# A quarter of the descriptor ring for GpSimd's transfers, and three more places for gathered rows

## The reference, cut to what matters

```python
def peer_ffn(x, w_pq, sub_keys, u_emb, v_emb):
    ...
        q = (xc @ w_pq).reshape(c, PEER_HEADS, 2, PEER_HALF)
        s = jnp.einsum('chpd,hpkd->chpk', q, sub_keys).astype(jnp.float32)
        sv, si = lax.top_k(s, PEER_TOPK)
        ...
        cv, ci = lax.top_k(cand, PEER_TOPK)
        eid = jnp.take_along_axis(cid, ci, axis=-1)
        gate = jax.nn.softmax(cv, axis=-1)
        act = jax.nn.gelu(jnp.einsum('chkd,cd->chk', u_emb[eid], xc), approximate=False)
        return jnp.einsum('chk,chkd->cd', (gate * act.astype(jnp.float32)).astype(xc.dtype), v_emb[eid])
```

## Time and profile before

| what | value |
|---|---|
| median of 3 runs | 1012.64 us (1012.56 to 1013.12) |
| span of the profiled execution | 1080.4 us |
| busy: PE, DVE, ACT, GpSimd | 69%, 64%, 37%, 58% of the span |
| TensorE clock granted, mean | 0.819 of full speed |
| read from HBM | 378.16 MB |
| first gather issued, last gather issued | 119.1 us, 1067.8 us |

### The profile page before, as it was taken

One profiled execution on the slowest core, in us unless ns is written; L12 is line 12 of the kernel. 1 busy time (PEld: TensorE's weight loads), 2 busy tenths in 40 slices (PEclk: granted clock), 3 DMA queues, 4 the chain that ended last, 5 costly groups with the idle time before them and its releaser, 6 DMA issues.

```text
span 1080.4 us, 13828 instructions
## 1 busy us (share of the span) xinstructions
PE 742.8 (69%) x4217; PEld 379.1 (35%) x4217; DVE 686.7 (64%) x1725; ACT 404.0 (37%) x1154; POOL 622.1 (58%) x584
## 2 busy tenths in 40 slices
PE   8999986554798677766536768757637567765444
PEld 3575834111354435543212233323213235231111
DVE  1363776997288543698695559988974535639542
ACT  1162142332356470333223346354516742322412
POOL 0000275777667765475565656766775665667664
PEclk9999997877778899988867878877778878887656
DMA  9924699999979999999899999999998999999997
GB/s 364 331 79 184 217 349 411 411 360 377 336 252 359 348 400 412 398 379 379 278 314 325 373 388 353 391 362 362 407 412 308 411 417 416 414 411 409 382 376 270
DMA packets 122443, 381.54 MB, mean 353 GB/s; under 512 B 16026, under 2 KB 40682, under 8 KB 117122
## 3 DMA queue, kind: packets, MB, share of 16 engines
q0 software_dynamic: 83696, 304.81, 74.0%
q1 hardware_dynamic: 38578, 75.78, 19.2%
q10 hardware_dynamic: 96, 0.07, 0.0%
HBM read 378.16 MB, written 4.14 MB: 354 GB/s over the span
## 4 chain that ended last, share of the span: by engine, by line
PE 28%; DVE 19%; issue 17%; ACT 10%; another core or an unknown queue 9%; DMA 8%; POOL 6%; SPq 3%; ACTq 0%; POOLq 0%; DVEq 0%
PE bank L463 17%; PE acc L463 9%; DVE rows L1453 6%; DMA w_uq_sb<-in_w_uq 3%; PE bank L466 3%; POOL rows L1978 3%; DMA rows<-in_peer_v,eid 2%; POOL rows L1996 2%; ACT spread L1101 2%; ACT L1092 1%; SPq L2069 1%; DVE shared L1793 1%; DVE shared L1782 1%; ACT shared L1063 1%
## 5 line engine op out<-in xcount | busy, mean ns | idle before, releaser
L463 PE MATMUL acc<-rows,spread 128*64 128x512 f32 (+1 forms) x1124 | 329.3, 682 | 143.9 <-ACT spread L1101 51.9
L1978 POOL DMA_INDIRECT rows<-in_peer_v,eid x254 | 275.8, 1086 | 160.5 <-issue 66.6
L1996 POOL DMA_INDIRECT rows<-in_peer_u,eid x184 | 193.2, 1050 | 109.0 <-issue 54.7
L463 PEld LDWEIGHTS acc<-rows,spread 128*64 128x64 f32 (+1 forms) x1124 | 89.1, 156 | 310.3 <-issue 240.2
L1453 DVE CUSTOM_DVE_ANT_0 rows<-rows,xr_even 128x1024 f32<-128x1024 f32 x89 | 108.1, 1218 | 34.0 <-DMA rows<-in_peer_u,eid 26.4
L1453 DVE CUSTOM_DVE_ANT_0 rows<-rows,xr_odd 128x1024 f32<-128x1024 f32 x95 | 116.2, 1223 | 19.6 <-DMA rows<-in_peer_u,eid 18.8
L1101 ACT ACTIVATE spread<-wide_consts,wts 128x64 f32<-128x64 f32 (+1 forms) x288 | 83.7, 337 | 35.2 <-remote 25.0
L1996 POOL DMA_INDIRECT first_u<-in_peer_u,eid x37 | 38.2, 1032 | 101.5 <-DVE eid L1835 81.6
L463 PE MATMUL acc<-more_v,spread 128*64 128x512 f32 (+1 forms) x140 | 73.6, 695 | 18.9 <-ACT spread L1101 9.9
L1094 ACT ACTIVATE wts<-gelus,gate 128x1 f32<-128x1 f32 x288 | 69.1, 287 | 4.7
L1063 ACT ACTIVATE shared<-bank 128x512 f32<-128x512 f32 (+4 forms) x68 | 27.8, 456 | 76.3 <-remote 35.5
(11 more groups left out here) (278 smaller groups left out, 1222.4 us busy)
## 6 DMA issues: line engine op xcount, KB each, us to landing
wring<-in_w_pq SPq DMA_DIRECT2D x12, 1024.0 KB
z<-in_w_pq SPq DMA_DIRECT2D x5, 1024.0 KB, 4.8
wring<-in_cache_ckv SPq DMA_DIRECT2D x40, 128.0 KB
rows<-in_w_in SPq DMA_DIRECT2D x2, 2048.0 KB, 15.2
rows<-in_w_pq SPq DMA_DIRECT2D x2, 2048.0 KB, 8.3
wring<-in_w_out SPq DMA_DIRECT2D x4, 1024.0 KB
wring<-in_cache_kv SPq DMA_DIRECT2D x32, 128.0 KB
rows<-in_peer_v,eid POOLq DMA_INDIRECT x254, 7.5
```

The costliest lines, as they stand in the source:

```text
L463: return T.matmul(o, lhsT=l, rhs=r, start=start, stop=stop, skip_group_check=True)
L1978: nc.gpsimd.indirect_dma_start(out=v_ring[V_PLACE[n]], out_offset=None, in_=inp["peer_v"], in_offset=bass.IndirectOffsetOnAxis(ap=eid[t][: ...
L1996: nc.gpsimd.indirect_dma_start(out=u_ring[U_PLACE[n]], out_offset=None, in_=inp["peer_u"], in_offset=bass.IndirectOffsetOnAxis(ap=eid[t][: ...
```

## The change

The ring of descriptors is 4096 bytes of every partition in place of 16,384. Of the 12,288 bytes, `u_ring` gets one more place (`RU` 7 to 8, a second `more_u`), `v_ring` two more (`RV` 9 to 11, a second and third `more_v`). Three tiles of one number per slot (`dots`, `gelus`, `wts`) grow from 16 to 24 columns, 96 bytes of a partition together, as more slots can be under way at once. Everything that is allocated in SBUF lies at other addresses. The first gathers into columns of `rows` are one u slot and two v slots later, and their waits move with them. Of the last slots, v of slot 284 no longer takes an x buffer but a place of the u ring.

```diff
--- before.py
+++ after.py
@@ -55,10 +55,11 @@
 SHARED = 4800
 NW = 2
 CW = 256
-RU, RV, RD = 7, 9, 4
+RU, RV, RD = 8, 11, 4
+SCRATCH = 4096
 PAIR = 2
 WIDE = 128 // PAIR
-RC = 8 * PAIR
+RC = 12 * PAIR
 GELU_LAG, SUM_LAG, V_LAG = 3, 6, 5
 
 
@@ -88,7 +89,7 @@
 V_USE = [n // RV for n in range(N_SLOTS)]
 V_LAST = [n - RV for n in range(N_SLOTS)]
 END_X, END_GUEST, END_ROW = N_SLOTS - 5, N_SLOTS - 4, N_SLOTS - 1
-V_END = {END_X: RU, END_GUEST: RU + 1, END_ROW: U_PLACE[N_SLOTS - 7]}
+V_END = {END_X: RU, END_GUEST: U_PLACE[N_SLOTS - 9], END_ROW: U_PLACE[N_SLOTS - 8]}
 for i, n in enumerate(V_END):
     V_PLACE[n], V_USE[n] = RV + i, 0
 for n in (N_SLOTS - 3, N_SLOTS - 2):
@@ -135,12 +136,12 @@
         w_uv = sb("w_uv_sb", [128, 2, NH * VD])
         keys_t = sb("keys_t", [128, 16, KEYS])
         bias_d = sb("bias_d", [128, NH, 256])
-        more_u = sb("more_u", [128, DM])
+        more_u = [sb(f"more_u{i}", [128, DM]) for i in range(2)]
 
         x_b = [sb(f"x{i}", [128, DM]) for i in range(2)]
         x = [x_b[t % 2] for t in range(3)]
         xr_odd = sb("xr_odd", [128, DM])
-        more_v = sb("more_v", [128, DM])
+        more_v = [sb(f"more_v{i}", [128, DM]) for i in range(3)]
         eid = [sb(f"eid{t}", [128, SLOTS[t]], U32) for t in range(3)]
         gate = [sb(f"gate{t}", [128, SLOTS[t]]) for t in range(3)]
         ckv_nat = sb("ckv_nat", [128, 3, KVL])
@@ -153,8 +154,8 @@
 
         rows = sb("rows", [128, 13, DM])
         rows_f = rows[:, :, :].rearrange("p a b -> p (a b)")
-        u_ring = [first_u[:, :], more_u[:, :]] + [rows[:, i, :] for i in range(5)] + [b[:, :] for b in x_b]
-        v_ring = [more_v[:, :]] + [rows[:, i, :] for i in (5, 6, 7, 8, 9, 10, 11, 12)]
+        u_ring = [first_u[:, :], *(b[:, :] for b in more_u)] + [rows[:, i, :] for i in range(5)] + [b[:, :] for b in x_b]
+        v_ring = [b[:, :] for b in more_v] + [rows[:, i, :] for i in (5, 6, 7, 8, 9, 10, 11, 12)]
         v_ring += [u_ring[p] for p in V_END.values()]
         spread = [sb(f"spread{i}", [128, PAIR, WIDE]) for i in range(RD)]
         dots = sb("dots", [128, RC])
@@ -266,7 +267,7 @@
         bias_df = bias_d[:, :, :].rearrange("p h k -> p (h k)")
         zs = [z, z, bias_df[0:32, 0:DIN]]
         z1_kept = xr_odd[:, 0:512]
-        loose = [first_u[:, :], more_u[:, :], more_v[:, :], g_fin[:, :]]
+        loose = [first_u[:, :], more_u[0][:, :], more_v[0][:, :], g_fin[:, :]]
         z2_kept = [f[:, :, :].rearrange("p a b -> p (a b)") for f in spread]
         junk = [z[:, 0:DM], shared[:, 0:DM], shared[0:32, 2 * DM:3 * DM]]
         x_root = [small[0:128, 5 + t:6 + t] for t in range(3)]
@@ -1965,9 +1966,9 @@
             def fetch_v(n):
 
                 t = [k for k in tiles if n >= BASE[k]][-1]
-                if n == 4:
+                if n == 6:
                     z1_done.wait(pool, 2)
-                if n == 8:
+                if n == 10:
                     z1_done.wait(pool, 3)
                 if n == END_X:
                     pool.wait_ge(sums_done, BASE[2] // PAIR + 1)
@@ -1985,8 +1986,8 @@
                     n = BASE[t] + j
                     if j in STARTS[t]:
                         pool.wait_ge(slots_ready, CHOSEN[t] + STARTS[t].index(j) + 1)
-                    if n in (2, 6):
-                        ready(pool, ("pq", {2: 1, 6: 2}[n], 0))
+                    if n in (3, 7):
+                        ready(pool, ("pq", {3: 1, 7: 2}[n], 0))
                     if n == U_GUESTS[0][0]:
                         pool.wait_ge(sums_done, 1)
                     if n == U_GUESTS[1][0]:
@@ -2296,7 +2297,7 @@
     import concourse.bacc as bacc
     from concourse.bass_utils import run_bass_kernel_spmd as run
 
-    nc = bacc.Bacc("TRN2", target_bir_lowering=False, num_devices=1)
+    nc = bacc.Bacc("TRN2", target_bir_lowering=False, num_devices=1, dynamic_dma_scratch_size=SCRATCH)
     arrays, inp, cst, out = {}, {}, {}, {}
     laid = laid_out(inputs)
     for name in INPUTS:
```

## The result

The changed kernel takes 1020.66 us (median of 5 runs, 1019.89 to 1021.05) against 1013.12 us of the kernel before (5 runs): ratio 1.0065, 95% interval 1.0049 to 1.0082. The medians differ by 7.5 us, and the interval is 5.0 to 8.3 us; 1003.9 us was forecast, with 986 to 1018 as the range.

A forecast was written before the change was run, and what follows sets the result against it. It took the limit to change by stage: row supply to 432 us and from 864, attention and expert choice between. Gains 1.2 + 5.0 + 0 + 2.5 + 0 = 8.7 us took 1012.6 to 1003.9 us; range 986 to 1018.

The forecast's parts named there:

- All this: 0: Waits added or moved, with the wider `dots`: no instruction added, covered by GpSimd's own stream, 0 us.
- the 24.9 us of stalls to 378 us: GpSimd's stalls for places from 135 to 378 us, the most that could come back there.
- the two gaps of the earlier trace: Gaps of 2.69 and 3.36 us before v gathers at the end, counted as waits for a place, expected to shrink.
- Start, 1.2 us: Start: one u gather goes ahead before each of two waits for query products; gain 1.2 us (0 to 2.5).
- More places to 378 us, 5.0 us: To 378 us: added places let gathers run ahead, two times one loop pass of 2.5 us; gain 5.0 us.
- 432 to 864 us, 0: From 432 to 864 us: stalls largest but worth nothing, as nobody waits for the rows; 0 us.
- End, 2.5 us: From 864 us to the end: two gaps before v gathers shrink; gain one pass, 2.5 us (0 to 9.4).
- Ring of descriptors, 0: The smaller descriptor ring costs 0 us, if a quarter of the old one holds all 20 places in flight.
- The first (no change): Whole kernel: the lead is given back, same bytes must come, end bound by DMA; 1012.6 us, chance 0.15.
- The second (larger): Both hungry stages: stalls were the loop's latency and all go; 35.5 us gained, 977 us, chance 0.12.
- the third (ring drains): Descriptor ring fills, GpSimd waits for landings: some 100 us, 1113 us less the gain; chance 0.08.
- The fourth (queueing ahead of SyncE's loads, about 1020 us): More gathers delay weight chunks or cache pages PE waits for: +7.6 us without gain, about 1020 us, chance 0.08.

The follow-up runs named there:

- after_al: The kernel after with an unused tile of 160 bytes behind `wts`, so later tiles start on multiples of 256 bytes again: 1011.26 us, ratio 0.9967 against the kernel before.
- rc24: The kernel before with the 4 KB ring and 24 columns of `dots`, `gelus` and `wts`, no new places: 1024.6 us, ratio 1.0104.
- the repeated profile: The kernel before, unchanged, profiled a second time: 1014.12 us (one run), span 1012.3 us.
- u8_al: The kernel before with one more u place (8 u, 9 v), 4 KB ring, 24 columns and 160 unused bytes behind `wts`: 1013.11 us, ratio 0.9997.
- after_all_al: The kernel after with unused tiles of 160, 32 and 224 bytes, so row places, weights and keys also start on multiples of 256: 998.64 us, ratio 0.9857.

## Why the prediction was wrong

**The step that failed** is "The wider `dots` (24 columns) costs no instruction ... All this: 0". It costs no instruction and no wait that any run shows, and it costs 9.4 us (1020.66 to 1011.26, where `after_al` keeps the 24 columns), since it moves the tiles behind it off multiples of 256 bytes. The prediction asked of each edit what it does to the order of instructions and to waits, and of none what it does to addresses. The diff and the list of tiles would have told: 3 x 32 bytes more ahead of the weight ring, `z` and the scratch, where SyncE's loads land. From two runs that are not the whole change the sum is -3.3 per mille for the places (`after_al`) and +10.4 for the columns (`rc24`), 7.1 per mille slower; 6.5 were measured.

**What bounds the kernel** was read wrong, from a profile 67.8 us over the timed median. The prediction noted the gap, and took the difference over unscaled. It should have asked which of the views could hold in an execution 6.7% too long. The rows gave a second sign: waits on "remote" and a chain with 9% of "another core or an unknown queue", where about half of the semaphore events are missing. "From 432 to 864 they hardly do ... Rows lie ready" was an artefact of this profile: with the repeated one PE waits 45.8 us for v rows in that stretch, 43.1 of them in `rows`. And the 24.9 us of stalls to 378 us are 2.6 in the repeated profile (243 - 187.0 - 178 x 0.30), whose 216 to 324 us move 400 GB/s and not 331, and the two gaps of the earlier trace rows are not there. A kernel at a DMA share of 1.02 to 1.04 has hardly a stall to give back. So three of the signs that the prediction named for being right came (waits for sums below 14.7 us, more than 331 GB/s, no gaps), and the kernel was slower: the repeated profile of before has them too. The fourth, shorter waits for rows from 216 to 432 us, didn't come by the first profile: PE 16.6 for 16.9 us and DVE 26.5 for 16.8.

**By its steps.**
- *Start, 1.2 us:* the two waits fell as described, by 1.2 and 1.5 us against the repeated profile. Its worth in the time wasn't measured alone; `u8_al`, which has the first of the two moved as in the kernel after, shows no gain.
- *More places to 378 us, 5.0 us:* right in kind, mis-sized. From 216 to 324 us GB/s rose from 400 to 408, 2.1 us. GpSimd's waits for sums from 216 to 432 fell from 14.7 (10.6 repeated) to 7.2 us.
- *432 to 864 us, 0:* wrong in its reason (rows do not lie ready), and the term wasn't 0: from 459 to 864 us the 9 us were lost, to the starts.
- *End, 2.5 us:* wrong. The gaps are in the first profile alone; the last landing takes 17.6 us before and 20.5 after, so the end is bound by the transfers in both. All places together bring about 3 us (ratio 0.9967) for the 8.7 forecast.
- *Ring of descriptors, 0:* right; ratio 1.0000 (0.9984 to 1.0016).

**The rivals.** The first (no change), at 0.15, had part of the mechanism that holds: the same bytes must come, and the end is bound by DMA. Its middle stage "paced by others" isn't so. With the starts as before its time would have been nearly right (1012.6 against 1011.26 us). Its rule of the Trainium skill (DMA: Bandwidth & Descriptors, "Where 436 GB/s comes from") of about 358 GB/s is not what binds this kernel on its one core: 385 GB/s over the span of `after_all_al` and its window of 419 show that. The second (larger) and the third (ring drains) are out. The fourth (queueing ahead of SyncE's loads, about 1020 us) named the measured time by luck, with another mechanism: `after_al` has all three places and their gathers in flight, and is faster than before. PE's waits for pages in `wring` over the span are 13.6 us before (repeated) and 14.4 after, far from 7.6 more.

**What stays open.** Why packets of the gathers get slower (162 to 166 ns) when only the destinations of the loads have moved. It happens only beside loads, so it is something that both share, but no run here takes it apart. Which property of a start off 256 bytes costs the time is not shown either, and starts beyond 96 bytes past a multiple were not tried. And why the first profile's execution was slow.

## What to carry to other kernels

Where the DMA share stands near 1, count the bytes of every tile that a change adds or widens, and look where the tiles behind it start: a tile of 32 unused bytes cost 12 us, and 256 placed well brought 13. Before a profile is read for stalls, set its span against the timed median; 6.7% apart, its waits were not those of the runs that are timed. Compare before and after by profiles that both stand near their medians. A wait that goes may only have moved: add up all waits of the engine, and not those of one line. And when each half of a change is slower than the whole, look for what all of them share.

## What the runs showed of the hardware that was not expected

- The start of a tile in the on-chip memory changes the rate of the transfers into it, at the same packets: with weight ring, scratch and z at 32, 64 or 96 bytes past a multiple of 256 the kernel takes 1.3, 1.2 and 1.0% more.
- With the rows' places on multiples of 256 as well, the stretch from 864 to 972 us moves 419 GB/s; with them at 64 past one it moves 408 or 409, in every kernel (the first profile of before, at another stage of its work there, has 415).
- The slow-down spreads: from 216 to 972 us gathers whose own places haven't moved last 168.5 ns for 164.3 beside loads with shifted destinations, and 163.8 for 164.7 where no load runs.
- A ring of descriptors of a quarter of the size costs nothing measurable with the places of before (ratio 1.0000), and with 19 places, where a row lands 17 us after its issue, the kernel is still faster than before once the starts are right.
